# First expert's rows by 0/1 matmuls instead of a gather, selection in two parts, logits from the residual

## The reference

```
x = x + W_out[ conv | pooling | spatial gating ](RMSNorm(x, norm1_g) @ W_in)
t = RMSNorm(x, norm2_g)
lc = t @ rc_w + rc_b                      # 4 groups
g_sel = argmax(lc);  p_sel = softmax(lc)[g_sel]
lf = (t @ rf_w + rf_b)[group g_sel]       # 8 experts of that group
top_v, top_i = top_k(lf, 2);  top_w = softmax(top_v)
y = sum over the two experts e:  p_sel * top_w * (silu(t @ w_gate[e]) * (t @ w_up[e])) @ w_down[e]
x = x + y;  out = RMSNorm(x, final_norm_g)
```

## Time and profile before

| | |
|---|---|
| median of 3 runs | 704.45 us (703.61 to 705.2) |
| the profiled execution, own time | 703.53 us |
| its span, first to last instruction | 701.7 us |
| TensorE busy | 661.7 us (94%) |
| VectorE / ScalarE / GpSimd busy | 300.9 / 111.1 / 45.7 us |
| moved by DMA | 229.82 MB, mean 328 GB/s |

### The profile page before, as it was taken

One profiled execution on the slowest core, in us unless ns is written; L12 is line 12 of the kernel. 1 busy time (PEld: TensorE's weight loads), 2 busy tenths in 40 slices (PEclk: granted clock), 3 DMA queues, 4 the chain that ended last, 5 costly groups with the idle time before them and its releaser, 6 DMA issues.

```text
span 701.7 us, 8819 instructions
## 1 busy us (share of the span) xinstructions
PE 661.7 (94%) x3762; PEld 370.3 (53%) x3762; DVE 300.9 (43%) x536; ACT 111.1 (16%) x203; POOL 45.7 (7%) x48
## 2 busy tenths in 40 slices
PE   7999999999988999999999999999999999999982
PEld 4999999887864343443434434434344333334331
DVE  4646238612438243344435433443243433324337
ACT  6421253301320001000000000010000010000005
POOL 2000000000002010001000100010000100000001
PEclk9999999999989999999999999999999999999997
DMA  9940600088148999999999999999999999999953
GB/s 287 336 144 3 240 1 1 1 345 328 78 187 336 412 420 418 421 420 419 417 418 420 420 419 419 420 420 417 419 420 419 418 420 418 420 421 420 418 207 135
DMA packets 45515, 229.82 MB, mean 328 GB/s; under 512 B 7876, under 2 KB 15061, under 8 KB 21155
## 3 DMA queue, kind: packets, MB, share of 16 engines
q1 hardware_dynamic: 42915, 224.52, 79.4%
q0 software_dynamic: 2560, 4.73, 1.9%
HBM read 228.03 MB, written 4.85 MB: 332 GB/s over the span
## 4 chain that ended last, share of the span: by engine, by line
PE 60%; DMA 17%; SPq 15%; DVE 5%; issue 1%; ACT 1%; POOLq 0%; DVEq 0%
PE ps L1501 17%; DMA w<-in_moe_w_up 16%; PE ps L1339 13%; SPq L492 10%; PE ps L1521 9%; PE ps L1410 8%; PE ps L1532 5%; SPq L498 5%; PE ps L1436 1%; PE ps L1512 1%; DVE hexT L1181 1%; DVE x_sb L831 1%; PE ps L1303 1%; PE ps L1305 1%; PE ps L1304 1%
## 5 line engine op out<-in xcount | busy, mean ns | idle before, releaser
L1501 PE MATMUL ps<-w,xT 128*64 128x512 f32 x1024 | 227.9, 593 | 12.0 <-DMA w<-in_moe_w_up 12.0
L1501 PEld LDWEIGHTS ps<-w,xT 128*64 128x64 f32 x1024 | 72.4, 137 | 161.7 <-issue 138.5
L831 DVE TENSOR_TENSOR x_sb<-ps,x_sb 128x512 f32<-128x512 f32 (+1 forms) x170 | 109.0, 682 | 45.4 <-PE ps L1410 32.7
L1521 PE MATMUL ps<-wd,hexT 128*64 128x512 f32 x512 | 116.9, 598 | 3.0 <-DVE hexT L1181 0.5
L831 DVE TENSOR_TENSOR hexp<-silu_g,ps 128x256 f32<-128x256 f32 x32 | 13.5, 421 | 194.3 <-ACT silu_g L789 194.3
L1521 PEld LDWEIGHTS ps<-wd,hexT 128*64 128x64 f32 x512 | 33.9, 136 | 65.4 <-issue 54.8
L1532 PE MATMUL ps<-y_hi,home 64*128 64x512 f32 (+1 forms) x320 | 66.4, 409 | 1.6 <-DVE y_lo L837 1.6
L1532 PE MATMUL ps<-y_lo,home 64*128 64x512 f32 (+1 forms) x320 | 63.2, 389 | 0.0
L595 POOL DMA_INDIRECT xg<-hn_rows,idx x32 | 36.0, 1124 | 371.8 <-PE ps L1491 353.6
L793 ACT ACTIVATE y_hi<-ps,gate_of 128x512 fp32r<-128x512 f32 x32 | 22.0, 688 | 211.5 <-PE ps L1521 211.5
L1339 PE MATMUL ps<-hT_hi,wi_hi 128*128 128x288 f32 x224 | 48.7, 299 | 0.0
(11 more groups left out here) (205 smaller groups left out, 575.1 us busy)
## 6 DMA issues: line engine op xcount, KB each, us to landing
wd<-in_moe_w_down SPq DMA_DIRECT2D x64, 1024.0 KB, 25.9
w<-in_moe_w_gate SPq DMA_DIRECT2D x63, 1024.0 KB, 25.7
w<-in_moe_w_up SPq DMA_DIRECT2D x63, 1024.0 KB, 26.8
wo<-in_w_out SPq DMA_DIRECT2D x2, 2048.0 KB, 10.8
x_sb<-in_x_prompt SPq DMA_DIRECT2D x4, 512.0 KB, 9.0
hn_rows<-hn2p SPq DMA_DIRECT2D x4, 512.0 KB, 2.7
out<-x_sb SPq DMA_DIRECT2D x4, 512.0 KB, 2.7
wi_v<-in_w_in SPq DMA_DIRECT2D x4, 384.0 KB, 8.1
```

Of the source, the lines that this page charges most:

```text
L831: return nc.vector.tensor_tensor(out, a, b, op)
L1501: last = mm(ps[64 * h:64 * h + 64, 1, :], lhs, w1[s][:, :, k, h * (F // 2):(h + 1) * (F // 2)], start=(k == 0), stop=(k == KD - 1))
L1521: last = mm(ps[64 * h:64 * h + 64, 3, :], lhs, wd[s][:, c, h * 512:(h + 1) * 512], start=(c == 0), stop=(c == F // P - 1))
```

## The change

1. Logits come from the residual. TensorE transposes `x_sb` instead of `hn2p` (`transpose_x2`), the router weights are multiplied by the gain beforehand (`rw` by `prmT`, so `rw` is loaded in another order, 16- and 128-byte runs), and `take_L` multiplies the logits by 1/rms. Transposes and logits of a tile move inside the W_out matmuls of the next tile (`between`).
2. The selection runs twice: `choose(0, 3)` for tiles 0 to 2 while the last tile of W_out is multiplied, `choose(3, 5)` for the rest.
3. Expert 0's rows come from matmuls: DVE makes `pick` (0/1 by place, times 1/rms), and `pick_rows` multiplies every eighth column of `x_sb` by it, 8 products for each tile, straight into the bank that held the transposes of the gathered rows. DVE multiplies by the gain (`g2p`) on the way to `xT`. GpSimd gathers for experts 1 and up.
4. Work moves behind the first `gate_up`: row numbers and gates of the 0/1 matmuls, spill blocks, the rows `hn2` of tile 4 and their store, the loads of `row_ids` and the final gain. `wd` of expert 2 no longer waits for gathered rows. The `stay_warm` matmuls of the routing are gone.

```diff
+            for j in range(NT - 1):
                 sp.wait_ge(hn2_ready, j + 1)
                 sp.dma_start(hn2_v[j * P:j * P + TOK[j], :], hn2p[0:TOK[j], j % 2, :]).then_inc(hn2_out[j % 2], 16)
-                if j == NT - 1:
-                    sp.dma_start(gain[:], final_g.rearrange("(o d) -> o d", o=1).broadcast_to([P, D])).then_inc(gf_in, 16)
             sp.wait_ge(wo_ps, 2 * NT)
...
             sp.wait_ge(L_ready, NT)
+            load_down(2, 2)
+            sp.wait_ge(hn2_ready, NT)
+            sp.dma_start(hn2_v[(NT - 1) * P:T, :], hn2_last).then_inc(hn2_out[0], 16)
             sp.dma_start(row_ids[:], consts[:, NKEPT:NCONST]).then_inc(rows_in, 16)
-            sp.wait_ge(xg_in[0], 16)
-            load_down(2, 2)
+            sp.dma_start(gain[:], final_g.rearrange("(o d) -> o d", o=1).broadcast_to([P, D])).then_inc(gf_in, 16)
...
+            add_mix(1, EARLY)
+            take_L(EARLY - 1)
+            choose(0, EARLY)
+            link(invert(EARLY))
+            dve.wait_ge(hn2_out[1], 16)
+            rows_hn2(EARLY, hn2p[:, 1, :])
+            add_mix(1, NT - 1)
...
+            choose(EARLY, NT)
+            pick_first(2)
...
+            place_onehots(0)
+            dve.wait_ge(main["xT_ps"], 1)
+            tt(xT[:].rearrange("p c (h s) -> p h c s", h=2),
+               ps[:, 0, :].rearrange("p (c h s) -> p h c s", c=4, h=2),
+               over(g2p[:].rearrange("p (h c) -> p h c", h=2)[:, :, :, None], [P, 2, 4, BLK]),
+               ALU.mult).then_inc(main["xT_ready"], 1)
+            place_onehots(1)
+            rows_hn2(NT - 1, hn2_last)
...
+            def pick_rows(a, b, turn):
+                pe.wait_ge(pick_ready, turn)
+                for j in range(a, b):
+                    n = TOK[j]
+                    for k in range(KD):
+                        at = (k % 4) * P + BLK * (k // 4)
+                        last = mm(ps[:, 0, at:at + BLK], x_sb[0:n, j, k:D:KD], pick[0:n, j, :], start=(j + k == 0),
+                                  stop=(j == NT - 1 and k == KD - 1))
+            places_early()
+            transpose_x2(NT - 1)
+            logits(NT - 1)
+            count_early()
+            pick_rows(0, EARLY, 1)
+            places_late()
+            pick_rows(EARLY, NT, 2)
```

More of the change, by code:

```diff
@@ L56 @@
 PO_A = 296
-R_CW, R_PS, R_SC, R_SP, R_ALL = 0, 9, 11, 17, 47
+R_CW, R_PS, R_SC, R_SP, R_G2, R_ALL = 0, 9, 11, 17, 47, 55
 BLK = 64
@@ L1029, in _, with invert, over @@
                 add_mix(0, j)
-            for j in range(NT):
-                n = TOK[j]
+            def invert(j):
+                dve.wait_ge(std2, j + 1)
+                return nc.vector.reciprocal(small[0:TOK[j], 5, j:j + 1], small[0:TOK[j], 4, j:j + 1])
+            mx, v1, v2, mark, mark_1, mark_2 = (small[:, c, :] for c in (9, 10, 11, 12, 24, 25))
+            psel, kdiff, kexp, w_hi = (small[:, c, :] for c in (13, 14, 15, 16))
+            first_rstd = small[:, 26, :]
+            def over(x, shape):
+                return x.broadcast_to(shape)
@@ L1032, in _ @@
+            for j in range(EARLY):
                 add_mix(1, j)
-                dve.wait_ge(std2, j + 1)
-                link(nc.vector.reciprocal(small[0:n, 5, j:j + 1], small[0:n, 4, j:j + 1]))
+                link(invert(j))
                 if j >= 2:
                     dve.wait_ge(hn2_out[j % 2], 16 * (j // 2))
[L1037 to L1041, removed]
@@ L1096, in _ @@
+            for (a, b), before in places_of:
+                last = tt(t_m[:, a:b], memb[:, a:b], over(before[:, :, None, :], [P, b - a, 2, NE]), ALU.mult)
+            link(last)
             link(nc.vector.tensor_reduce(place, t_c, AX.X, ALU.add))
-            dve.wait_ge(hn2_out[0], 48)
             dve.wait_ge(hn2_out[1], 32)
@@ L1390, in _, with output @@
             last.then_inc(st_ps, 1)
-            def output(half, *tiles):
+            def output(half, *tiles, between=nothing):
                 turns = [half * NT + j for j in tiles]
@@ L1462, in _, with between, run, count @@
-            pe.wait_ge(tri_ready, 1)
-            mm(ps[:, 7, 0:(NT + 1) * NE], tri_b[:], Mb[:].rearrange("p t e -> p (t e)"), start=True, stop=False)
+            def between(j):
+                def run(i):
+                    if i == 3 and j:
+                        transpose_x2(j - 1)
+                    if i == 6 and j:
+                        logits(j - 1)
+                return run
             for j in range(NT):
+                output(1, j, between=between(j))
+            def count(j, out, tiles, start=False, stop=False):
@@ new lines, in count_early, with places_late @@
+            def count_early():
+                for j in range(EARLY):
+                    count(j, ps[:, 5, 0:(NT + 1 - EARLY) * NE], NT + 1 - EARLY, start=(j == 0))
+            def places_late():
+                pe.wait_ge(memb_ready, 2)
+                mm(ps[:, 5, 0:(NT - EARLY) * NE], tri_b[:], Mb[:, EARLY:NT, :].rearrange("p t e -> p (t e)"), start=False,
+                   stop=False)
+                for j in range(EARLY, NT):
+                    last = count(j, ps[:, 5, (j + 1 - EARLY) * NE:(NT + 1 - EARLY) * NE], NT - j, stop=(j == NT - 1))
+                last.then_inc(pos_ps, 1)
```

271 lines of the change are left out of this document (149 added, 122 removed).

## The result

The changed kernel takes 712.75 us (median of 4 runs, 712.47 to 714.2) against 704.27 (4 runs): a ratio of 1.0124, interval 1.0106 to 1.0142. It is slower by 8.5 us, where 701.5 was forecast and 708.0 was the end of the range. The profiled execution took 712.79 (span 710.8) against 703.53 (701.7).

A forecast was written before the change was run, and what follows sets the result against it. The DMA weight stream, full at 419 GB/s from 225 to 665 us, was taken as the bound. Lost DMA time falling from 5.9 to 3.0 saves 2.9: 700.6 profiled, 701.5 median; range 700.0 to 708.0.

The forecast's parts named there:

- the price s of a pick: TensorE time per pick instruction, 80 in all, reading every eighth column: taken 0.12 us, bounds 0.106 and 0.195.
- the clock, kept apart as a rival: Rival 3: TensorE's clock falls to 0.50 around tile 4's transposes, adding 5.5 us on picks and logits: 707.0; chance 0.17.
- H: Time when SP issues expert 3's first weight piece; forecast at X + 5.1, against 227.20 in the kernel before.
- X: Start of the first expert's first `gate_up` on TensorE: forecast 207.75 + 80 s = 217.35, 6.2 us earlier than before.
- the ledger: DMA time lost from 201.5 to 225: 5.9 us before, 3.0 after, including 0.9 for bytes falling into the stretch anew.
- The case's own range: Spread of the main forecast alone, by the gain's cost and s down to 0.106: 700.3 to 702.4 us.
- the gain's 1.2 and the gap's 0.2: DMA losses forecast after the change: 1.2 us for slow store and gain, 0.2 for the dry queue before tile 4's rows.
- The DVE row: Evidence for the pick's upper bound: DVE at stride 8 takes 2.36 against 1.28, giving 0.195 us; doubled-read rival, chance 0.13.
- The `hexp` rows: Transposes reading every second column, load 207 ns against 141: 0.156 us a pick; as a rival 704.4 us, chance 0.17.
- the rule of the Trainium skill: SBUF lines are 16 bytes and each crossing pays a penalty: every element of a pick pays, a stride of two is free.
- the forecast's rule: Each us that the first `gate_up` starts past 217.4 is one more us of dry DMA queue.
- rivals 4 and 5: 4: expert 1's gathered rows late, first turn starves, 703.5, chance 0.04. 5: TensorE is the bound, 698.3, chance 0.02.

The follow-up runs named there:

- e10_order_warm_less: Changed kernel with picks of neighbouring columns, expert 0's gate and up weights loaded in matching row order, four filler matmuls: 701.87 us, 0.9946 of the kernel before.
- e9_order_warm: As e10_order_warm_less against the changed kernel, but five fillers, two instead of one ahead of tile 4's transposes: 701.93 us, 0.9955 of the kernel before.
- e7_warm_before_contig: Changed kernel with three fillers around tile 4's transposes and picks of neighbouring columns (expert 0's column order wrong): 706.13 us, 1.0009 of the kernel before.
- e3_warm_contig: Changed kernel with fillers around tile 4's transposes and among the picks, plus picks of neighbouring columns (wrong column order): 705.33 us, 1.0017 of the kernel before.
- e6_rows_warm: As e5_rows, with three filler matmuls around tile 4's transposes: 705.02 us, 1.0002 of the kernel before.
- e5_rows: Changed kernel with pick operands exchanged: 0/1 block stands, x_sb streams at a step of eight, rows then transposed: 704.23 us, 0.9988 of the kernel before.
- e2_contig: Changed kernel with picks reading 128 neighbouring columns (wrong column order for expert 0), no fillers: 709.98 us, 1.0099 of the kernel before.
- e12_strided_same: e10_order_warm_less with strided picks and the changed kernel's expert 0 weight order put back, same four fillers: 713.61 us, 1.0123 of the kernel before.
- e4_warm_before: Changed kernel with three filler matmuls around tile 4's transposes, none among the strided picks: 715.13 us, 1.0152 of the kernel before.
- e1_warm: Changed kernel with fillers around tile 4's transposes and behind the strided picks of tiles 0 to 3: 721.50 us, 1.0246 of the kernel before.
- e8_strides: Changed kernel with the fillers of e1_warm and picks of tiles 0 to 4 at column steps 1, 2, 4, 8, 8: 714.34 us, one run.

## Why the prediction was wrong

The step that failed is the price s of a pick, with an upper bound that was too low; the clock, kept apart as a rival and priced too low as well, came on top of it. The account of the DMA queue held.

The end follows H. Of each kernel's profiled execution (first `gate_up` X, H, us):

| kernel | us a pick | X | H | profiled us |
|---|---|---|---|---|
| e10_order_warm_less | 0.115 | 216.19 | 221.35 | 700.98 |
| e9_order_warm | 0.115 | 217.87 | 224.15 | 701.93 |
| e7_warm_before_contig | 0.115, late ones 0.154 | 217.82 | 224.78 | 702.57 |
| e3_warm_contig | 0.122 | 220.62 | 225.78 | 705.26 |
| e6_rows_warm | (wide) | 219.11 | 225.93 | 703.58 |
| before | (gather) | 223.50 | 227.20 | 703.53 |
| e5_rows | (wide) | 218.71 | 228.40 | 706.94 |
| e2_contig | 0.218 | 224.18 | 230.91 | 708.64 |
| e12_strided_same | 0.242 | 228.73 | 235.23 | 713.66 |
| after | 0.242 | 225.67 | 235.26 | 712.79 |
| e4_warm_before | 0.242 | 227.45 | 237.14 | 715.22 |
| e1_warm | 0.25 | 234.33 | 244.00 | 721.40 |

From e7_warm_before_contig to e1_warm H moves by 19.2 and the time by 18.8. The versions of the changed kernel lie within 0.8 us of 702.57 + (H - 224.78), but for e3_warm_contig (1.7 above: there tile 4's store and the small loads are issued only 2.3 us ahead of H, and 3.9 or more in the others, so I take it that they no longer fit into the gap; no run shows it apart) and e10_order_warm_less (1.8 above: its queue no longer runs dry, so H has ceased to count). The kernel before lies 1.5 below, 0.9 of which is the ledger's bytes. The times are those of the executions that the traces show, and not medians: e5_rows's is the slowest of twelve, e7_warm_before_contig's the fastest of ten.

Point by point:

- **What bounds the kernel, and the ledger: right.** DMA time lost before 240 accounts for 8.7 of the 9.1 us between the two spans. The case's own range does not quite add up: without the gain's 1.2 and the gap's 0.2 it begins at 700.1, and with 1.8 for the gain it ends at 702.1, not at 700.3 and 702.4; nothing hangs on it.
- **W_out's end (201.1), the front of the queue, the selections: right.** W_out ends at 200.9, weights issued at 201.29 (forecast 202), tile 3's rows at 200.9 (201.4), dry at 221 (221.0), selections of 4.95 and 4.6 (4.9 and 4.6).
- **The price s: wrong, and beyond its upper bound.** Taken 0.12, bounds 0.106 and 0.195, measured 0.242 and 0.252. The 80 took 19.7 us instead of 9.6, 10.1 more; X moved by 8.3, because they started at 204.18 and not at the 205.6 within the fixed 207.75 (tile 4 has 64 tokens, so its logits took 1.12, not 1.87). The step that failed is "Nearest in form are the logits": form and load count were the same, but the column step was eight, and the load itself grew from 192 ns to 335 at the same clock. That "the stride may cost little where the load is slow anyway" held at a step of two (198 ns) and failed at four and eight. The DVE row at the same step (a factor 1.84 by its longest, 1.73 by its medians) was the nearer one, and 2.0 is what came. The `hexp` rows, at a step of two, were no step between the two: e8_strides shows that a step of two costs a pick next to nothing. Whether their 207 ns against 141 is the step after all, hidden in a pick by a load that is slow anyway, or has another cause, is open. It was those rows that I set against the rule of the Trainium skill, and for the picks the rule was right.
- **The clock: a rival at 0.17, and it came as well.** It was low from 204.3 to 235.0. In the changed kernel and in e2_contig it fell at 204.3 and 203.5, 0.1 us behind the first pick and 1.1 ahead of it, and behind TensorE's waits of 0.7 and 0.6 around tile 4's transposes, where the rival had it; with fillers there (e4_warm_before) it fell at 208.3. Its price was read from mixed forms, 0.058 more for each pick; contiguous picks at 0.50 cost 0.218, 0.1 more. Strided picks pay nothing for it (4.03 us for 16 at 1.00, 3.86 at 0.50). For them it cost elsewhere: H stands 9.6 behind X, not 5.1, so 4.5 us in the first expert's first half, whose first eight instructions took 3.68 instead of 1.94 in e10_order_warm_less. I had counted the rivals as exclusive; 8.3 for X and 4.5 for H - X make 12.8, and 12.2 came. Either mechanism alone would have left the range, which ended at 708.0: an X that is 8.3 later makes 709.8 by the forecast's rule (no run has strided picks at 1.00 throughout), and the low clock without the stride is e2_contig, 709.98.
- **"Dense picks" as an argument against the clock: wrong.** In e4_warm_before the clock held through transposes and logits and fell inside the picks, without any gap. By the Trainium skill (TensorE: Matmul & The Clock Gate, Part 4) a transpose does not count as busy for the clock the way other matmuls do; no run here separates that, since fillers stood on both sides of the transposes or nowhere.
- **Gathers and the first turn (rivals 4 and 5):** H to the next first piece took 14.5 us, 12.8 before. The forecast allowed for it: expert 1 at X + 16 and its first piece 3.7 later, as before, make 14.6 behind X + 5.1. Since expert 1's rows come later, its transposes stand behind the down products (244.53 behind 240.94, with 0.85 of wait for `xT`), where before they were done ahead of them (232.20 and 232.88). With the queue already late this cost nothing that can be seen; in e10_order_warm_less expert 1's transposes do wait 1.29 for gathered rows, while the DMA share stays at 1.01.

Left open: what in a stream of picks lets the clock fall, why the same kernel keeps it in some runs and not in others (e7_warm_before_contig), and why e9_order_warm lost it where e10_order_warm_less, with a filler less, did not.

## What to carry to other kernels

A new operand has two prices, its shape and its access pattern; the row to bound it by is the one with the same column step, on whatever engine. A step of four float32 columns or more about doubled an instruction here. Rivals listed apart need not exclude each other: either of these two alone was enough to leave the range, and mending only one (e2_contig) gave back little. Lay out the data that is loaded from memory anyway (here expert 0's weights) so that the operand on the critical path is read in neighbouring columns: together with four fillers for the clock, that turned a loss of 8.5 us into a gain of some 3.5.

## What was not expected of the hardware

- Either operand pays about twofold for a column step of eight: the standing one 0.242 us an instruction against 0.115, the moving one 0.475 for 512 columns against 0.224 in `gate_up`, which has the same form.
- The price of the standing one jumps between a step of two and four: 2.00 and 3.72 us for 16 instructions, 198 and 330 ns for a load.
- Strided picks take the same at either clock level, 4.03 us for 16 at 1.00 and 3.86 at 0.50; 48 contiguous ones take 5.54 and 10.47.
- TensorE's clock fell under an unbroken stream of picks: TensorE 1.00 busy in every us from 206 to 210 in e1_warm, and the granted clock went from 1.00 to 0.50 in the fourth of them.
